# A fused encoder layer with routed experts on one core: routing searched in all expert groups at once with prefix sums by doubling, and a new order of the vector and scalar work inside an expert

## What is computed

```python
p_group = softmax(t @ w_rg + b_rg)            # 4 groups
top_p, top_g = top_k(p_group, 1)
group_onehot = one_hot(top_g[:, 0], 4)
inner_logits = einsum('td,gde->tge', t, w_re) + b_re      # 4 experts in each group
sel_logits = einsum('tge,tg->te', inner_logits, group_onehot)
top_l, top_e = top_k(sel_logits, 2)
top_w = softmax(top_l)
inner_gate = einsum('tk,tke->te', top_w, one_hot(top_e, 4))
gate = (group_onehot * top_p)[:, :, None] * inner_gate[:, None, :]
for e in range(16):
    a, u = split(t @ w_ei[e], 2)              # 1024 x 1024
    y = y + gate[:, e:e + 1] * ((silu(a) * u) @ w_eo[e])  # 512 x 1024
```

## Time and profile before

| | |
|---|---|
| median of 3 runs | 1425.87 us (1424.17 to 1425.99) |
| profiled execution, its own time | 1428.31 us |
| its span, first to last instruction | 1426.6 us |
| busy: PE, PEld, DVE, ACT, POOL | 90%, 75%, 53%, 45%, 19% |
| mean granted TensorE clock | 0.952 |

### The profile page before, as it was taken

How to read it: one execution, slowest core, us unless ns; L and a number is a source line. 1 busy time by engine, 2 the same in 40 slices (tenths; PEclk the granted TensorE clock), 3 DMA queues, 4 the chain that set the end, 5 groups by cost and what they waited for, 6 DMA issues and landing times.

```text
span 1426.6 us, 20185 instructions
## 1 busy us (share of the span) xinstructions
PE 1290.1 (90%) x7662; PEld 1074.5 (75%) x7663; DVE 754.0 (53%) x957; ACT 645.9 (45%) x878; POOL 270.2 (19%) x279
## 2 busy tenths in 40 slices
PE   5999899999998999999999896488999999999970
PEld 5788767788798888766788796466787778778860
DVE  3333367222654333367212655478855776885556
ACT  3222476332312322466332313367745564875445
POOL 0432000000300332000000300234522433652220
PEclk9999999999999999999999997589999999999995
DMA  7774400144662544300144653289977977996426
GB/s 188 226 169 89 89 1 2 29 90 131 141 201 89 112 96 89 89 2 1 27 93 124 142 207 142 101 269 280 355 218 227 339 248 263 312 378 218 145 74 241
DMA packets 58177, 222.40 MB, mean 156 GB/s; under 512 B 11800, under 2 KB 12312, under 8 KB 50648
## 3 DMA queue, kind: packets, MB, share of 16 engines
q1 hardware_dynamic: 42800, 177.38, 42.0%
q0 software_dynamic: 12192, 34.51, 8.6%
q10 hardware_dynamic: 3116, 9.54, 1.8%
HBM read 200.17 MB, written 34.32 MB: 164 GB/s over the span
## 4 chain that ended last, share of the span: by engine, by line
PE 78%; DVE 8%; issue 6%; ACT 5%; DMA 2%; POOL 1%; ACTq 0%; POOLq 0%; DVEq 0%; SPq 0%
PE banks L660 21%; PE banks L661 20%; PE banks L662 20%; PE banks L830 2%; PE banks L794 2%; PE banks L865 2%; PE banks L944 2%; ACT moe_hi L1211 2%; PE banks L872 1%; DVE moe_lo L1360 1%; PE banks L805 1%; DVE h_full L1706 1%; POOL gated L569 1%; PE banks L969 1%; DMA raw<-in_front_w 1%
## 5 line engine op out<-in xcount | busy, mean ns | idle before, releaser
L1360 DVE TENSOR_TENSOR moe_lo<-moe_raw,moe_hi 128x2048 fp32r<-128x2048 f32 x102 | 233.1, 2289 | 79.5 <-ACT moe_hi L1211 79.1
L1373 DVE TENSOR_TENSOR wlo<-raw,whi 128x2048 fp32r<-128x2048 f32 (+1 forms) x52 | 116.1, 2233 | 185.1 <-ACT whi L1053 185.1
L1211 ACT ACTIVATE moe_hi<-moe_raw 128x2048 fp32r<-128x2048 f32 x102 | 194.7, 1913 | 42.2 <-PE banks L662 39.9
L660 PE MATMUL banks<-xT,whi 128*128 128x512 f32 x448 | 175.4, 391 | 0.0
L661 PE MATMUL banks<-xT,whi 128*128 128x512 f32 x448 | 174.8, 390 | 0.0
L662 PE MATMUL banks<-xT,wlo 128*128 128x512 f32 x448 | 174.8, 390 | 0.0
L660 PE MATMUL banks<-wlo,xT 128*128 128x256 f32 x512 | 149.1, 291 | 8.3 <-DVE xT L1503 7.0
L660 PE MATMUL banks<-moe_lo,xeh 128*128 128x512 f32 x368 | 148.8, 404 | 8.3 <-issue 3.8
L661 PE MATMUL banks<-whi,xT 128*128 128x256 f32 x512 | 146.6, 286 | 0.0
L662 PE MATMUL banks<-whi,xT 128*128 128x256 f32 x512 | 146.5, 286 | 0.0
L661 PE MATMUL banks<-moe_hi,xeh 128*128 128x512 f32 x368 | 145.9, 396 | 0.0
(11 more groups left out here) (244 smaller groups left out, 2394.0 us busy)
## 6 DMA issues: line engine op xcount, KB each, us to landing
moe_raw<-in_expert_w SPq DMA_DIRECT2D x192, 512.0 KB
raw<-in_front_w SPq DMA_DIRECT2D x104, 512.0 KB, 6.8
toeplitz_rows<-bias_rows POOLq DMA_DIRECT2D x4, 1152.0 KB, 15.5
kqv<-in_x SPq DMA_DIRECT2D x8, 512.0 KB, 10.7
pt<-in_x SPq DMA_DIRECT2D x2, 2048.0 KB, 9.4
x_rows<-pt ACTq DMA_DIRECT2D x8, 512.0 KB, 2.7
token_sums<-pt ACTq DMA_DIRECT2D x8, 512.0 KB, 3.6
sum_tile<-token_sums SPq DMA_DIRECT2D x8, 512.0 KB, 6.9
```

The source lines that it names most:

```text
L660: mm(dst, left[0], right[1], start=first, stop=False)
L1211: A(moe_hi[m % SPLIT_E], moe_raw[m % RAW_E], ACT.Copy).then_inc(e_hi, 1)
L1360: V.tensor_tensor(moe_lo[m % SPLIT_E], moe_raw[m % RAW_E], moe_hi[m % SPLIT_E].bitcast(F32), ALU.subtract).then_inc(e_lo, 1)
L1373: V.tensor_tensor(view(lo, shape), view(raw[c % 2], shape), view(hi, shape).bitcast(F32), ALU.subtract).then_inc(w_split, 1)
```

## The change

It has two parts. In the **routing**:

- The ACT queue splits chunk 0 before the last `store_x1` and chunk 1 before the last `keep_x1`. DVE splits only chunks 0 and 1 before the last logits, and chunks 2 and 3 after the tables.
- The search runs over the four experts of all four groups at once (128 numbers per partition), side by side with the search for the group; waits are placed by hand (`run`, `done`) so that two independent chains alternate. The sums over preceding blocks are three additions of shifted 128-wide views over zeroed margins. PE starts its first rank product as soon as the membership is there, and `ranked` is signalled after the second product.
- The slot's column is found from the rank by shifts of two 16-wide integers, and the pass by one more, in place of comparisons over 128 columns.
- The one-hots are made in halves, first choices before second ones, and ACT and PE begin with the first half. `hot_col` and `hot_token` are in the one-pass 32-bit format, so the first table takes one pass of PE; the second one (gates) takes the same as before. The gates are made by DVE after the one-hots, and the count of passes after the first table.
- POOL issues the gathers for the second expert only when those for the first have landed. `rt` is wider (2560 columns) and lies elsewhere.

In the **experts' loop** the work of half 1 on both engines stands ahead of a split: on DVE `gated_half(1)` and `acts_lo(1)` ahead of split +2, and `rows_lo` part 1 ahead of split +3; on ACT `acts_hi(1)` ahead of split +3. The core of the diff:

```diff
-NOWHERE = 4 * MAXTOK
+NOWHERE = MAXTOK
...
-            nc.alloc_sbuf_tensor_at(name, [P, 2 * NT * P], F32, offset=place_at)[:, :].rearrange("p (n i) -> p n i", n=2 * NT)
-            for name, place_at in (("hot_lo", hot_at), ("hot_gate", hot_at + W_BYTES),
-                                   ("hot_col", late_at), ("hot_token", late_at + W_BYTES))]
+            nc.alloc_sbuf_tensor_at(name, [P, 2 * NT * P], dt, offset=place_at)[:, :].rearrange("p (n i) -> p n i", n=2 * NT)
+            for name, dt, place_at in (("hot_lo", F32, hot_at), ("hot_gate", F32, hot_at + W_BYTES),
+                                       ("hot_col", F32R, late_at), ("hot_token", F32R, late_at + W_BYTES))]
...
             for b in range(2):
+                if b == 1:
+                    pool.wait_ge(rows_in[0], 32)
...
-            mm(bank[2][:, 0:M16], before, rt[:, 0:M16], start=True, stop=False)
-            mm(bank[2][:, 0:M16], ones, rt[:, M16:2 * M16], start=False, stop=True)
-            mm(bank[3][:, 0:NE], ones, rt[:, 2 * M16:2 * M16 + NE], start=True, stop=True).then_inc(ranked, 1)
+            mm(bank[2][:, 0:M16], before, member_t, start=True, stop=False)
+            pe.wait_ge(member, 2)
+            mm(bank[2][:, 0:M16], ones, upto_t, start=False, stop=True).then_inc(ranked, 1)
+            mm(bank[3][:, 0:NE], ones, upto_t[:, M16 - NE:M16], start=True, stop=True).then_inc(ranked, 1)
             for a in range(2):
                 for n in range(2 * NT):
-                    pe.wait_ge(hot_ready, 2)
+                    pe.wait_ge(hot_ready, 2 + 2 * (n // NT))
                     pe.wait_ge(weighted, 2 * NT * a + n + 1)
-                    last = mm(bank[4 + a][:, 0:FULL_COL], hot_w[a][:, n], hot_col[:, n], start=(n == 0), stop=(n == 2 * NT - 1))
+                    last = mm(bank[4 + a][:, 0:FULL_COL], hot_w[a][:, n], hot_col[:, n] if a == 0 else hot_col[:, n].bitcast(F32),
+                              start=(n == 0), stop=(n == 2 * NT - 1))
                 last.then_inc(tabled, 1)
...
-                if s == SEQS - 1:
-                    store_x1(s, 3)
-                    keep_x1(s, 3)
...
-            for c in range(EARLY_E):
-                e_split(0, c)
+            e_split(0, 0)
+            store_x1(SEQS - 1, 3)
+            e_split(0, 1)
+            keep_x1(SEQS - 1, 3)
+            e_split(0, 2)
...
             for k, weight in enumerate((token, gate)):
-                act.wait_ge(hot_ready, 1)
                 for n in range(2 * NT):
+                    act.wait_ge(hot_ready, 1 + 2 * (n // NT))
+                    if k == 1:
+                        act.wait_ge(gates_made, 1)
...
                         gated_half(1)
+                        acts_hi(1)
                         e_split(pair, b * ECH + 3 + SPLIT_E)
-                        acts_hi(1)
...
-                    for c in range(EARLY_E):
-                        e_split(0, c)
+                    for o in (0, R_PAIRS - 4 * NE, R_FOURS - 4 * NE):
+                        V.memset(rt[:, o:o + 4 * NE], 0.0).then_inc(zeroed, 1)
+                    V.memset(small[:, 58:60], 0.0)
+                    e_split(0, 0)
+                    e_split(0, 1)
                     logit(s, 2)
                     logit(s, 3)
...
+            n_e = run(V.tensor_reduce(t4(best), lg_e, X, ALU.max))
+            n_g = run(V.tensor_reduce(g_max, lg_g, X, ALU.max))
+            done(n_e)
+            n_e = run(V.tensor_tensor(t44(e_tmp), lg_e, over_e(best), ALU.is_equal))
+            done(n_g)
+            n_g = run(V.tensor_tensor(t4(g_tmp), lg_g, over_4(g_max), ALU.is_equal))
+            V.tensor_tensor(t4(g4), lg_g, over_4(g_max), ALU.subtract).then_inc(r_exp_in, 1)
+            done(n_e)
+            n_e = run(V.tensor_tensor(t44(e_tmp), t44(e_tmp), tie_e, ALU.mult))
+            done(n_g)
+            n_g = run(V.tensor_tensor(t4(g_tmp), t4(g_tmp), tie_g, ALU.mult))
+            done(n_e)
+            n_e = run(V.tensor_reduce(t4(e_tie), t44(e_tmp), X, ALU.max))
+            done(n_g)
+            n_g = run(V.tensor_reduce(g_tie, t4(g_tmp), X, ALU.max))
+            done(n_e)
+            n_e = run(V.tensor_tensor(t44(hot1), t44(e_tmp), over_e(e_tie), ALU.is_equal))
+            done(n_g)
+            n_g = run(V.tensor_tensor(t4(g_hot), t4(g_tmp), over_4(g_tie), ALU.is_equal))
+            done(n_e)
+            chain(V.scalar_tensor_tensor(t44(rest), t44(hot1), NEG, lg_e, ALU.mult, ALU.add))
+            chain(V.tensor_reduce(t4(second), t44(rest), X, ALU.max))
+            n_e = run(V.tensor_tensor(t44(e_tmp), t44(rest), over_e(second), ALU.is_equal))
+            n_g = run(V.tensor_tensor(t4(g_tmp), t4(second), t4(best), ALU.subtract))
+            done(n_e)
+            n_e = run(V.tensor_tensor(t44(e_tmp), t44(e_tmp), tie_e, ALU.mult))
+            done(n_g)
+            n_g = run(V.tensor_tensor(t4(g_tmp), t4(g_tmp), t4(g_hot), ALU.mult))
+            done(n_e)
+            n_e = run(V.tensor_reduce(t4(e_tie), t44(e_tmp), X, ALU.max))
+            done(n_g)
+            V.tensor_reduce(e2, t4(g_tmp), X, ALU.add).then_inc(r_exp_in, 1)
+            done(n_e)
+            chain(V.tensor_tensor(t44(hot2), t44(e_tmp), over_e(e_tie), ALU.is_equal))
+            chain(V.tensor_tensor(e_tmp, hot1, hot2, ALU.add))
+            V.tensor_tensor(t44(member_t), t44(e_tmp), over_e(g_hot), ALU.mult).then_inc(member, 1)
+            dve.wait_ge(zeroed, 3)
+            dve.wait_ge(member, 1)
+            pairs, fours = rt[:, R_PAIRS:R_PAIRS + M16], rt[:, R_FOURS:R_FOURS + M16]
+            chain(V.tensor_tensor(pairs, member_t, rt[:, R_MEMBER - NE:R_MEMBER - NE + M16], ALU.add))
+            chain(V.tensor_tensor(fours, pairs, rt[:, R_PAIRS - 2 * NE:R_PAIRS - 2 * NE + M16], ALU.add))
+            V.tensor_tensor(upto_t, fours, rt[:, R_FOURS - 4 * NE:R_FOURS - 4 * NE + M16], ALU.add).then_inc(member, 1)
+            V.tensor_tensor(t44(one1), t44(hot1), over_e(g_hot), ALU.mult)
+            chain(V.tensor_tensor(t44(one2), t44(hot2), over_e(g_hot), ALU.mult))
+            prod, base = r(2 * M16), r(2 * NT)
+            chain(V.tensor_tensor(by_expert(prod), by_expert(ones12), expert_base.unsqueeze(1).broadcast_to([P, 2 * NT, NE]), ALU.mult))
+            chain(V.tensor_reduce(base, by_expert(prod), X, ALU.add))
...
+            chain(V.tensor_tensor(prod.rearrange("p (k m) -> p k m", k=2), ones12.rearrange("p (k m) -> p k m", k=2),
+                                  bank[2][:, 0:M16].unsqueeze(1).broadcast_to([P, 2, M16]), ALU.mult))
+            chain(V.tensor_reduce(rank, by_expert(prod), X, ALU.add))
+            chain(V.tensor_copy(rank_i, rank))
+            n_lo = run(V.tensor_scalar(lo_i, rank_i, P - 1, None, ALU.bitwise_and))
+            n_col = run(V.tensor_scalar(col_i, rank_i, 7, None, ALU.logical_shift_right))
+            n_over = run(V.tensor_scalar(pass_i, rank_i, 8, None, ALU.logical_shift_right))
+            done(n_lo)
+            n_lo = run(V.tensor_copy(lo_f, lo_i))
+            done(n_col)
+            n_col = run(V.tensor_copy(col_f, col_i))
+            done(n_over)
+            chain(V.tensor_copy(pass_f, pass_i))
+            n_col = run(V.scalar_tensor_tensor(col_f, pass_f, float((NE - 1) * SLOTS // P), col_f, ALU.mult, ALU.add))
...
+            def one_hot(hot, number, k):
+                part = slice(k * NT, (k + 1) * NT)
+                V.tensor_tensor(hot[:, part], iota.unsqueeze(1).broadcast_to([P, NT, P]),
+                                number[:, part].unsqueeze(2).broadcast_to([P, NT, P]), ALU.is_equal).then_inc(hot_ready, 1)
+            done(n_lo)
+            one_hot(hot_lo, lo_f, 0)
+            done(n_col)
+            chain(V.scalar_tensor_tensor(col_f, base, 1.0 / P, col_f, ALU.mult, ALU.add))
+            one_hot(hot_col, col_f, 0)
+            one_hot(hot_lo, lo_f, 1)
+            one_hot(hot_col, col_f, 1)
+            dve.wait_ge(r_exp, 2)
...
+            V.tensor_tensor(gate[:, NT:2 * NT], gate[:, 0:NT], e2, ALU.mult).then_inc(gates_made, 1)
...
+            dve.wait_ge(tabled, 1)
+            chain(V.tensor_scalar(slot_v[:, 0:FULL_COL, 1], bank[4][:, 0:FULL_COL], float(NOWHERE), None, ALU.add))
+            V.tensor_scalar(slot_v[:, 0:FULL_COL, 0], slot_v[:, 0:FULL_COL, 1], MAXTOK - 1, None, ALU.bitwise_and).then_inc(table_ready, 1)
+            dve.wait_ge(ranked, 2)
...
-            for c in range(EARLY_E, RAW_E):
+            for c in range(2, RAW_E):
...
                         e_split(pair, b * ECH + 1 + SPLIT_E)
                         acts_lo(0)
                         rows_lo(1 - b, z + 1, 0)
-                        e_split(pair, b * ECH + 2 + SPLIT_E)
                         gated_half(1)
                         acts_lo(1)
+                        e_split(pair, b * ECH + 2 + SPLIT_E)
+                        rows_lo(1 - b, z + 1, 1)
                         e_split(pair, b * ECH + 3 + SPLIT_E)
-                        rows_lo(1 - b, z + 1, 1)
                         e_split(pair, b * ECH + 4 + SPLIT_E)
```

132 lines of the change are left out of this document (52 added, 80 removed).

## The result

The changed kernel takes 1410.74 us (median of 4 runs, 1409.34 to 1412.82), the one before 1425.38 us beside it; the ratio is 0.9897 (0.9881 to 0.9914). That is 14.6 us less: faster, as forecast, but 5.7 us less of it than the predicted 1405.0 would have been. Its profiled execution has a span of 1408.8 us, against 1426.6.

What follows compares the result with a forecast made beforehand. The prediction took the routing to be one chain with nothing beside it, and DVE and DMA to be nearly full in narrow expert steps. Routing -14.5 and experts -6.4 gave -20.9, from median 1425.87 to 1405.0 us; range 1400.5 to 1415.

Steps and rivals of the forecast that it cites:

- the first rival: Experts' loop gives nothing back, as VectorE or the DMA engines bound narrow steps; routing's 14.5 us alone, 1411.4 us; chance 0.28.
- The start: Routing up to the first reduction: earlier splits on ACT and fewer on DVE bring that reduction forward, -4.6 us.
- Search, rank to one-hots, halves and tables: Routing from first reduction to DVE's table instruction: alternating chains -2.0, shifts for comparisons -2.8, half one-hots and one-pass table -4.5 us.
- The gather: Routing's wait for the first gathered rows: holding back the second expert's gathers, against more reloads beside it, -0.6 us.
- The bound of -17.5: Best case for the whole routing, in us: the gather at -3, the rest as summed.
- The experts: Experts' loop: the new order of work gains in narrow steps, nothing in wide ones, -6.4 us in all.
- The mechanism at half 1: Narrow steps: DVE makes `h_full` before a low part, so nine PE waits of 1.37 us each, 12.4 together, go.
- nets 0.5 by carrying the lateness through: Consecutive narrow steps 10 to 12: DVE's 0.9 us lateness is paid at the next half 0, leaving 0.5 us gained.
- the first of the signs of being wrong: Experts' loop: DVE late at half 0 of narrow steps behind narrow ones, by more than 1 us.
- steps 0 and 1 gain 1.37 each: First two narrow steps of the experts' loop: each gains the full 1.37 us since DVE idles in them.
- The slower case by late raw buffers: Late low part +2 delays reloads, each of nine narrow steps grows by 3.4 us; 1442 us; chance 0.04.
- another of the prediction's signs: Experts' loop: ACT or PE waiting for `moe_raw`, the raw weight chunks, would show the forecast wrong; no size given.

Runs made afterwards that it cites:

- experiment 7: The changed kernel with the routing's start as before (ACT stores and keeps the last rows before its splits, DVE makes three low parts before the last logits): 1414.29 us.
- experiment 3: The changed kernel without POOL's wait for the first expert's rows before it issues the second expert's gathers: 1405.44 us.
- experiment 4: Two kernels with half of each weight chunk's load left out from the second buffer pass on: changed kernel, 1406.99 us; new routing with old loop order, 1405.53 us.
- experiment 1: The changed kernel with both engines' loop programs as before, so the new routing alone: 1416.02 us.
- experiment 2: The kernel before with the new order in both engines' expert loops, so the old routing stays: 1420.40 us.
- experiment 5: The changed kernel with DVE's split +2 moved between the half-1 product and its low part: 1413.25 us with full loads, 1407.27 with half loads.
- experiment 10: The changed kernel with low part +2 cut in two halves around the half-1 product and POOL's hold on the second expert's gathers removed: 1411.02 us.
- experiment 6: The changed kernel with DVE's low part +2 cut in two column halves, one before and one behind the half-1 product: 1412.14 us.

## Why the prediction was right, and where it was off

The range held the time, and both parts of the change gained, as forecast. But the number is not the forecast's: 1410.7 lies 0.7 us from the first rival's 1411.4 and 5.7 us from 1405.0. That agreement with the rival is chance, since it has 14.5 us of the routing and nothing of the loop, where the times show 9.3 and 3.9 to 5.4. Had I left out the 3.2 us of the clock, the same working would have given 1408.2. By its steps:

- **The start**, -4.6: the trace shows -4.7, but 1.7 of it was the clock of the one execution that I took the rows from. At equal clock it is -3.0 in T (experiment 7, whose times put 4.4 us on the whole). I took ACT's late start (877.05) as the kernel's own; the 3.13 us of the `route` matmuls ahead of it, in a window at 0.76, was there to be read.
- **Search, rank to one-hots, halves and tables**, -9.3 together: T to `slot_tab` went from 24.55 to 15.46, -9.1. Each landmark is within 0.3 us of where it was put, the 0.29 us for a 128-wide reduction and the one-pass table included. At equal clock the tables bring 1.4 less.
- **The gather**, -0.6: it came out at +0.5. The terms that failed are the value of holding the queue back (0.1 us at the rows, experiment 3) and the price of the reloads beside the gather, which I named and left out of the sum: one fewer brings the rows 1.3 us earlier (experiment 7), halved ones 2.1 (experiment 4). The bound of -17.5 is also added up wrong: with the gather at -3 and the rest as summed it is -16.9.
- **The experts**, -6.4: the profile shows -2.1, in which the order gives -4.0 to -5.0 and 1.9 to 2.9 come back with the new routing (experiments 1 and 2); timed, the order has -3.9 to -5.4. The mechanism at half 1 was right: nine waits gone, isolated steps at 1.1 to 1.2 for 1.37. One sub-term failed: that the run 10 to 12 "nets 0.5 by carrying the lateness through": it lost 2.7. DVE reaches half 0 of the second and third step not 0.9 us late but so late that PE waits 2, and PE pays twice, by the wait and by the lower clock behind it. This is the first of the signs of being wrong that the prediction named. On another, that steps 0 and 1 gain 1.37 each "since DVE idles in them", the profiles don't agree: 1.0 together against the kernel before, 3.5 against experiment 1, 5.3 between the kernel before and experiment 2. DVE's idle time there is in part a wait for late chunks, and a low part of DVE ends inside the stop before step 1 (3.1 us into it in the changed kernel, 1.9 in its second profile, 2.0 before).
- **The rivals.** "The loop gives nothing back" had the right place, and part of its price: narrow steps behind narrow ones. Its reason was half wrong. It is not the DMA engines at 0.98 (experiment 4), but DVE's own standing time; they come in only once that is cured (experiments 5 and 10). The slower case by late raw buffers did not come: ACT's waits for chunks, another of the prediction's signs, grew by 8.4 us over the run, and isolated steps still gained.

What stays open: why a version that saves 4 us in steps 10 to 12 is not faster in its median, what the stops before steps 1 and 2 are, and whether the kernel without the hold is faster. The profiles show several us of scatter ahead of the root and in steps 0 to 2, but runs without a profile can't be cut at these places.

## What to carry to other kernels

Before you subtract two durations of one profile, look at the granted clock in the windows on the path: here 3 us of a 14 us estimate were a clock that fell 2 us earlier in that one execution. Where an engine is nearly full, an instruction moved ahead of its input turns into standing time, and the next step pays for it; in a run of such steps it adds up, so put something short in front of the wait (half of the low part here) rather than nothing. And time a version over several runs, beside the one that it is compared with, before you believe a profile of it: 4 us in one place of a profile vanished in the median (experiment 6), and 4 us in the medians were not in the profiles (experiment 7).

## What the runs showed of the hardware

- Behind a wait of 2.06 us PE's next work ran at the lower of its two clocks, 1.2 in place of 2.4 GHz (granted 0.57 in the 4 us from 1222.4, 1.00 in the 4 us ahead of them, of which PE was busy 1.9). In experiment 6, behind waits of 1.8 us, with PE busy 2.2 of the 4 us ahead, it did not.
- With PE equally busy (3.81 of 4 us), the clock fell within the first 4 us behind the root in one execution and not in another.
- Ahead of steps 1 and 2 PE stands for 1.2 to 5.3 us, of which up to 3.2 us (experiment 1) have nothing to wait for in the trace. Two packets of an instruction queue, 1 to 2 us each, start near each of these stops, and in the changed kernel's experts none starts after that, but no run shows them to be the cause.
- The first two gathers took 9.7 us from the start of their second issue beside full chunk reloads and 7.6 beside half ones. With the other two gathers on the same queue behind them it was 9.6 (experiment 3).
